# Output-projection products spread over the last steps of a first attention, gate products spread further over a second, and a weight split in two pieces

## The reference, cut to what matters

```
first block:
  xn = rms_norm(x) ; proj = xn @ w_in -> qa ka va za | qi ki wi | qb kb vb zb
  a_out = attention over the 128 keys that an indexer picks (8 heads of 64)
  b_out = dilated attention (8 heads of 64)
  mixed = concat(a_out * silu(za), b_out * silu(zb))
  x = x + mixed @ w_out
second block:
  h = rms_norm(x) ; proj = h @ w_in_2 -> q, kv, gates, pool input, g_merge
  a = nsa_attention(...) @ w_branch_attn       # compressed + selected + window
  b = pool_mixer(...) @ w_branch_pool
  ga, gb = split(sigmoid(g_merge))
  x = x + (ga * a + gb * b) @ w_out_2
  x = x + square(relu(rms_norm(x) @ w_ff1)) @ w_ff2 ; rms_norm
```

## Time and profile before

| what | before |
|---|---|
| median of 3 runs | 1055.77 us (1055.59 to 1056.2) |
| the profiled execution | 1055.27 us |
| its span, first to last instruction | 1053.5 us |
| PE busy | 1038.2 us (99% of the span) |
| DVE / ACT / POOL busy | 650.9 / 517.2 / 341.9 us (62% / 49% / 32%) |
| mean DMA rate | 139 GB/s |
| mean granted TensorE clock | 0.998 |

### The profile page before, as it was taken

The page is one execution under the profiler, slowest core; times in us unless marked ns, Lnnn a source line. Parts: engine busy times, 40 slices in busy tenths (PEclk is TensorE's granted clock), DMA queues, the critical chain, the costliest instruction groups (busy, mean ns, idle before and its releaser), DMA issues. The chain is left out here.

```text
span 1053.5 us, 14396 instructions
## 1 busy us (share of the span) xinstructions
PE 1038.2 (99%) x5362; PEld 851.5 (81%) x5362; DVE 650.9 (62%) x1149; ACT 517.2 (49%) x929; POOL 341.9 (32%) x329
## 2 busy tenths in 40 slices
PE   9999999999999999999999999999999999999997
PEld 7788887888778898988777778888888888888885
DVE  5578997676775333514567778444222325999976
ACT  8453345554562343344467874134433436554554
POOL 0022110004310003700155430008679954753542
PEclk9999999999999999999999999999999999999999
DMA  8654323223320375133200362239999942443542
GB/s 329 116 124 107 100 80 78 64 62 120 132 91 1 108 242 158 41 80 81 60 2 2 108 233 60 81 100 338 341 345 335 333 163 61 150 137 133 199 180 81
DMA packets 99639, 146.26 MB, mean 139 GB/s; under 512 B 6209, under 2 KB 60225, under 8 KB 99569
## 3 DMA queue, kind: packets, MB, share of 16 engines
q1 hardware_dynamic: 86016, 129.70, 37.9%
q10 hardware_dynamic: 12768, 12.88, 3.8%
q0 software_dynamic: 784, 2.75, 1.7%
HBM read 123.69 MB, written 21.63 MB: 138 GB/s over the span
## 5 line engine op out<-in xcount | busy, mean ns | idle before, releaser
L2319 DVE TENSOR_TENSOR w_lo<-wring,w_hi 128x1024 fp32r<-128x1024 f32 x32 | 50.6, 1582 | 110.4 <-ACT w_hi L1732 110.4
L1878 DVE TENSOR_TENSOR u_lo<-wring,u_hi 128x1024 fp32r<-128x1024 f32 (+1 forms) x64 | 78.8, 1240 | 53.0 <-ACT u_hi L1469 52.5
L842 PE MATMUL bank<-u_hi,h_hi 128*128 128x512 f32 (+1 forms) x288 | 110.9, 385 | 0.1
L842 PE MATMUL bank<-u_hi,h_lo 128*128 128x512 f32 (+1 forms) x288 | 109.2, 379 | 0.0
L842 PE MATMUL bank<-u_lo,h_hi 128*128 128x512 f32 (+1 forms) x288 | 109.0, 378 | 0.0
L1469 ACT ACTIVATE u_hi<-wring 128x1024 fp32r<-128x1024 f32 (+1 forms) x64 | 65.8, 1032 | 82.8 <-PE bank L842 70.3
L842 PE MATMUL bank<-h_hi,w_lo 128*128 128x512 f32 (+2 forms) x272 | 104.5, 384 | 0.0
L842 PE MATMUL bank<-h_hi,w_hi 128*128 128x512 f32 (+2 forms) x272 | 104.4, 384 | 0.0
L842 PE MATMUL bank<-h_lo,w_hi 128*128 128x512 f32 (+2 forms) x272 | 104.3, 384 | 0.0
L842 PE MATMUL bank<-h_hi,u_hi 128*128 128x512 f32 x224 | 95.0, 424 | 0.3 <-ACT arena L1411 0.2
L1303 PE MATMUL bank<-s_hi,f_hi 128*128 128x512 f32 x224 | 88.5, 395 | 0.1
(11 more groups left out here) (349 smaller groups left out, 2478.8 us busy)
## 6 DMA issues: line engine op xcount, KB each, us to landing
wring<-in_w_in SPq DMA_DIRECT2D x60, 512.0 KB, 3.9
wring<-in_w_ff ACTq DMA_DIRECT2D x12, 1024.0 KB, 8.5
wring<-sums_kept SPq DMA_DIRECT2D x16, 768.0 KB, 4.3
wring<-in_w_ff SPq DMA_DIRECT2D x22, 512.0 KB, 6.1
wring<-in_w_ff SPq DMA_DIRECT2D x32, 256.0 KB, 3.3
sums_kept<-wring SPq DMA_DIRECT2D x22, 256.0 KB, 5.2
arena<-in_w_out SPq DMA_DIRECT2D x4, 1024.0 KB, 5.1
wring<-in_w_out SPq DMA_DIRECT2D x2, 2048.0 KB, 13.6
```

What stands on the lines that cost most here:

```text
L842: last = mm(b, lhs, rhs, start=(start and n == 0), stop=(stop and n == 2))
L1878: v.tensor_tensor(u_lo[u % RAW_UNITS][:, 0:cols], raw_unit(u), u_hi[u % HI_UNITS][:, 0:cols].bitcast(F32), ALU.subtract).then_inc(u_lo_don ...
L2319: v.tensor_tensor(cut(w_lo[ring3(m)]), src, cut(w_hi[ring3(m)]).bitcast(F32), ALU.subtract).then_inc(w_lo_done, 1)
```

## The change

It edits five things.

1. **First attention, PE.** Sixteen products of i = 0 (eight for each half n) leave the place behind the last step. Seven of them go into the pairs t = 58 to 66 (`ROW_AT`), behind the scores and ahead of turns and values; one goes ahead of the last output's transposes, the other eight behind them, in an order that keeps those that need the last outputs late (`first_row`).
2. **First block's weight splits.** The parts 5 to 8 of `WO` get their low split on POOL, behind its last `combo`, and no longer on DVE; ACT makes their high splits earlier (59, 61, 63 and right behind the last step), and that of part 9 ahead of the last mixed high split.
3. **Gate projection of the second block.** The last products of `gb` are stretched: the last four stand in the pairs t = 52, 54, 56, 58 in place of 48, 50, 52, 54.
4. **Branch weight splits.** The high splits of e = 0 and 1 on ACT go from behind steps 59 and 62 to behind 61 and 63. The low split of e = 0 on POOL goes from u = 59 to two pieces of 512 columns, at u = 61 and at u = 63; each counts one, so a product with e now waits for e + 2.
5. **Branch products.** The last two products of `branch_product(1)` move ahead of the wait for the attention's low splits.

```diff
--- before.py
+++ after.py
@@ -190,7 +190,7 @@
     FILL2 = [("gb", e) for e in range(2, 8)]
     fill1 = [(m * 7 // 8, FILL1[m // KC], m % KC) for m in range(KC * len(FILL1))]
     GB2_FRONT = 3
-    fill2 = [(m - GB2_FRONT if m < 32 else 32 + (m - 32) * 4 // 3 if m < 44 else 2 * m - 40, FILL2[m // KC], m % KC)
+    fill2 = [(m - GB2_FRONT if m < 32 else 32 + (m - 32) * 3 // 2 if m < 44 else 2 * m - 36, FILL2[m // KC], m % KC)
              for m in range(GB2_FRONT, KC * len(FILL2))]
     filled = {tile: t for t, tile, k in fill1 if k == KC - 1}
 
@@ -199,11 +199,12 @@
 
     SILU_STEP = [filled[FILL1[2 * n + 1]] for n in range(4)]
     WO = [(0, 0, 2), (0, 2, 2), (0, 4, 1), (0, 5, 1), (0, 6, 1), (0, 7, 1)] + [(1, k, 1) for k in (4, 5, 6, 7, 0, 1, 2, 3)]
-    WO_HIGH = {46: 0, 48: 1, 50: 2, 53: 3, 55: 4, 60: 5, 62: 6}
+    WO_HIGH = {46: 0, 48: 1, 50: 2, 53: 3, 55: 4, 59: 5, 61: 6, 63: 7}
     MIXED = [4, 5, 6, 7, 0, 1, 2, 3]
+    ROW_AT = {58: ((0, 0),), 60: ((0, 1),), 62: ((0, 2),), 64: ((0, 4), (0, 5)), 66: ((0, 3), (1, 0))}
     ROUNDS = TOPK // 8 * (NT - 1)
     GB_HIGH = {9 * n + 7: unit_of[("gb", 6 + n)] for n in range(2)}
-    BRANCH_HIGH = {59: 0, 62: 1}
+    BRANCH_HIGH = {61: 0, 63: 1}
 
 
     A1 = [("qi", 0), ("qi", 1), ("ki", 0)]
@@ -1020,6 +1021,31 @@
                     last = nc.tensor.transpose(b[:, i * P:(i + 1) * P], qk1[:, o // 4, o % 4, OUTS, i * P:(i + 1) * P], ident)
                 last.then_inc(t_full, 1)
 
+            def product1(b, i, n, j):
+                k = MIXED[j]
+                at, c = mix_place(k)
+                return three(b, (wo_high_of(n, k)[:, 0, :], wo_low_of(n, k)[:, 0, :]), slice(0, 512),
+                             (qk1_half[:, at, c, MIX_HI, :], qk1_half[:, at, c, MIX_LO, :]), slice(i * P, (i + 1) * P),
+                             False, j == 0, j == KC - 1)
+
+            def row1(n, j):
+                k = MIXED[j]
+                if j == 0:
+                    pe.wait_ge(a_free, A1_END)
+                pe.wait_ge(mixed_lo_done, j + 1)
+                pe.wait_ge(wo_lo_done, [m for m, (half, c, count) in enumerate(WO) if half == n and c <= k < c + count][0] + 1)
+                return product1(bank[n][:, :], 0, n, j)
+
+            def first_row():
+                row1(1, 1)
+                mixed_transposes(NS // NH - 1)
+                row1(0, 6)
+                row1(1, 2)
+                row1(0, 7).then_inc(r_full, 1)
+                for j in range(3, KC):
+                    last = row1(1, j)
+                last.then_inc(r_full, 1)
+
             pe.wait_ge(t_free, TT[("qk", "qb", 3)] + 1)
             pe.wait_ge(rel_free, IDX_HEADS * (NT - 1))
             for t in range(0, NS + 4, 2):
@@ -1031,6 +1057,8 @@
                     pair1(t)
                     fill(fill1, t)
                     fill(fill1, t + 1)
+                for n, j in ROW_AT.get(t, ()):
+                    row1(n, j)
                 if t % NH == 2 and t >= 18:
                     mixed_transposes((t - 18) // NH)
                 for n in range(2):
@@ -1038,13 +1066,13 @@
                         turn1(t - 2 + n)
                     if 4 <= t:
                         value1(t - 4 + n)
-            mixed_transposes(NS // NH - 1)
-            pe.wait_ge(a_free, A1_END)
-            pe.wait_ge(o_free, NS // NH)
-
-            def residual(r0, ready, product, then):
+
+            def residual(r0, ready, product, then, first_row=None):
 
                 for i in range(NT):
+                    if i == 0 and first_row is not None:
+                        first_row()
+                        continue
                     for n in range(2):
                         if n == 1 and i >= 1:
                             then(i - 1)
@@ -1058,22 +1086,7 @@
 
             h2 = lambda i: h_transposes("h2", xn2, NT, [i])
 
-            def ready1(i, n):
-                if i == 0 and n == 0:
-                    pe.wait_ge(wo_lo_done, 6)
-
-            def product1(b, i, n, j):
-                k = MIXED[j]
-                at, c = mix_place(k)
-                if i == 0 and n == 0:
-                    pe.wait_ge(mixed_lo_done, j + 1)
-                if i == 0 and n == 1:
-                    pe.wait_ge(wo_lo_done, 7 + j)
-                return three(b, (wo_high_of(n, k)[:, 0, :], wo_low_of(n, k)[:, 0, :]), slice(0, 512),
-                             (qk1_half[:, at, c, MIX_HI, :], qk1_half[:, at, c, MIX_LO, :]), slice(i * P, (i + 1) * P),
-                             False, j == 0, j == KC - 1)
-
-            residual(0, ready1, product1, h2)
+            residual(0, lambda i, n: None, product1, h2, first_row)
 
 
             nat_unit("kv2", 0, tiles=[0, 1, 2])
@@ -1217,7 +1230,7 @@
 
             def branch_product(at, chunks=range(4)):
                 e, n = BRANCH[at]
-                pe.wait_ge(br_lo_done, e + 1)
+                pe.wait_ge(br_lo_done, e + 2)
                 if at >= 4:
                     pe.wait_ge(r_free, 2 * NT + at - 3)
                 act = (a_hi, a_lo) if n == 0 else (pm_hi, pm_lo)
@@ -1245,10 +1258,9 @@
                     branch_product(0)
                 if t == NS + 2:
                     branch_product(1, range(2))
+            branch_product(1, range(2, 4))
             pe.wait_ge(at_lo_done, NT - 1)
             for half in range(2):
-                if half == 1:
-                    branch_product(1, range(2, 4))
                 pe.wait_ge(last_lo_done, half + 1)
                 for at in (2, 3):
                     branch_product(at, range(2 * half, 2 * half + 2))
@@ -1592,10 +1604,11 @@
                     mixed_high((t - 19) // NH)
                 if t in WO_HIGH:
                     wo_high(WO_HIGH[t])
+            wo_high(8)
             mixed_high(6)
-            wo_high(7)
+            wo_high(9)
             mixed_high(7)
-            for m in range(8, 14):
+            for m in range(10, 14):
                 wo_high(m)
             for u in range(HI_UNITS):
                 high(U2 + u)
@@ -2071,13 +2084,14 @@
                 for u in (t, t + 1):
                     if u in LOW1:
                         low(LOW1[u])
-                    if u - 2 in WO_HIGH:
+                    if WO_HIGH.get(u - 2, 5) < 5:
                         wo_low(WO_HIGH[u - 2])
             mixed_low(6)
-            wo_low(7)
             mix(7)
+            dve.wait_ge(wo_lo_done, 9)
+            wo_low(9)
             mixed_low(7)
-            for m in range(8, 14):
+            for m in range(10, 14):
                 wo_low(m)
             for u in range(2):
                 low(U2 + u)
@@ -2290,7 +2304,7 @@
                     if u - 3 in GB_HIGH:
                         low(GB_HIGH[u - 3])
                 if t == NS:
-                    dve.wait_ge(br_lo_done, 1)
+                    dve.wait_ge(br_lo_done, 2)
                     branch_low(1)
                 if t == NS + 4:
                     gate(0)
@@ -2469,6 +2483,13 @@
                 g.tensor_tensor(combo[c % 2][:, 0:(i + 1) * P], strips[:, h, (NT - 1 - i) * P:S], mask_of[i], ALU.add)\
                     .then_inc(combo_done, 1)
 
+            for m in range(5, 9):
+                n, k, count = WO[m]
+                pool.wait_ge(wo_lo_done, m)
+                pool.wait_ge(wo_hi_done, m + 1)
+                g.tensor_tensor(wo_low_of(n, k, count), wo_raw(n, k, count), wo_high_of(n, k, count).bitcast(F32), ALU.subtract)\
+                    .then_inc(wo_lo_done, 1)
+
             pool.wait_ge(xn_done, NT)
             pool.wait_ge(r_full, R_BRANCH)
             pool.wait_ge(t_free, TT[("mx", NS // NH - 1)] + 1)
@@ -2519,10 +2540,11 @@
                         .then_inc(pm_lo_done, 1)
                 if u >= 15 and u % NH == NH - 1:
                     add_turned((u - 15) // NH)
-                if u == 59:
+                if u in (61, 63):
                     pool.wait_ge(br_hi_done, 1)
-                    g.tensor_tensor(br_lo[0][:, :], wring[:, branch_at[0]:branch_at[0] + UNIT], br_hi[0][:, :].bitcast(F32), ALU.subtract)\
-                        .then_inc(br_lo_done, 1)
+                    part = slice((u - 61) * 256, (u - 61) * 256 + 512)
+                    g.tensor_tensor(br_lo[0][:, part], wring[:, branch_at[0]:branch_at[0] + UNIT][:, part], br_hi[0][:, part].bitcast(F32),
+                                    ALU.subtract).then_inc(br_lo_done, 1)
 
             def side_totals(j):
                 pool.wait_ge(a_free, AT[("ff", 2 * j + 1)] + 1)
```

## The result

| | before | after |
|---|---|---|
| median | 1055.76 us (1055.42 to 1056.49, 6 runs) | 1060.67 us (1059.63 to 1061.46, 6 runs) |
| profiled execution, its span | 1055.27, 1053.5 | 1060.80, 1059.0 |
| mean granted clock of TensorE | 0.998 | 0.995 |

The change makes the kernel slower: the ratio is 1.0046 with an interval of 1.0034 to 1.0058, so 4.9 us (3.6 to 6.1). The prediction was 1060.0 in a range of 1056.9 to 1062.6.

The account below looks back on a forecast made before the run. PE was taken to bound the kernel, so only its idle time can be won. -1.7 (first attention) + 4.2 (second) + 1.7 (clock) = +4.2 us on 1055.27, 1059.5; median 1060.0, range 1056.9 to 1062.6.

Parts of the forecast that it names:

- first attention: End of the first attention: products fill PE's waits, 3.27 to 1.25 us; less 0.3 at the norm, 1.7 us gained.
- first branch product late: Second attention: PE waits for POOL's second piece behind output 6's addition; product starts at 617.2, not 612.46, 4.75 us late.
- wait of 0.53 filled: Second attention, at 620.12: two branch products moved ahead of the attention's low splits fill PE's wait, gain 0.53 us.
- clock: Behind the 5.9 us gap of PE: granted clock falls to half for 3.5 us, costing 1.75 us.
- those of 0.23 and twice 0.15: First attention, waits of PE left: 0.23 at t = 58, 0.15 for the transposes, 0.15 for the split of output 6.
- What the norm takes back: Norm of query block 0: block ready at 315.5, PE there at 315.2, giving back 0.3 us.
- The wait of 0.51: Second attention, at 603.66: PE's wait is filled by the stretched gate products, counted as 0.3 us.
- the 0.82: Second attention: PE's wait for POOL's scaling of steps 60 and 61 goes, as no branch split stands ahead of it.
- the rival of 0.28: Behind the same stall of PE, the clock holds or returns within a few matmuls: +2.5, 1058.3 us; chance 0.28.
- The branch weights: Rival, second attention: weights land at 609.5, ACT's chain and the second piece come 2 us later, 1062.0 us; chance 0.12.
- The short stall: Rival, second attention: ACT's chain runs on PE's lead, piece done before about 614.5, 1055.0 or 1053.5 us; chance 0.08.
- That the first attention gives nothing: Rival: DVE's chain sets the first attention's end, gain 0 and not 1.7, so 1061.7 us; chance 0.07.

Follow-up runs that it names:

- the first part alone: Points 1 and 2 of the change only, second attention, its fill work and branch splits as before: 1054.03 us, 0.9984 to the kernel before.
- the two kernels with one of the two undone: Points 1 and 2 only, against 1054.03 us: low splits 5 to 8 back on DVE, 1054.26 us; or no first-row products among the attention's steps, 1055.61 us.
- the second part alone: Points 3, 4 and 5 of the change only, first attention as before: 1061.99 us, 1.0060 to the kernel before.
- the unused matmuls: Changed kernel with 24 matmuls of 128 by 512, results never used, ahead of the first branch product: 1059.58 us, 1.0038 to the kernel before.
- the kernel with the short gap: Changed kernel with POOL's second piece of the branch split ahead of the addition of output 6: 1056.17 us, 1.0002 to the kernel before.

## Why the prediction was right

The mechanism was the one forecast: the stall, what it waits for, the clock behind it and the smaller gain ahead. The sizes of its terms compare so:

| term | predicted | measured |
|---|---|---|
| first attention | -1.7 | -1.64 by medians, -2.14 between the profiled executions |
| first branch product late | +4.75 | +5.23 |
| wait of 0.53 filled | -0.53 | gone from the trace |
| clock | +1.75 | +2.04 in the trace, 1.1 by medians |

By the traces this sums to +4.6, against the +4.2 forecast and +4.9 by medians. The late product and the clock cost 0.48 and 0.29 us more than forecast, and the first attention gave 0.44 more, so the errors cancel in part: that the total came within 0.7 us is in part luck.

- *First attention.* The waits went from 3.27 to 0.57, further than the 1.25 predicted: those of 0.23 and twice 0.15 that I left standing are not there, and the last one is 0.57 for 0.72. Of these 2.70 us, 2.22 reach the second row of products (1.38 earlier, 0.84 late at the start); no wait in the profile names the rest. What the norm takes back is not fixed by this code: of the seven traces with this first row, four have no wait at the norm, as the changed kernel's, and three one of 0.25 to 0.42. That is why the first part alone gives 1.64 in its trace (0.86 early at the norm, 0.78 late at the start) and the same code 2.14 in the other. That the products and not the splits do it is shown by the two kernels with one of the two undone.
- *The late branch product.* The order on POOL was read rightly: the sum on DVE, the addition, 0.72 us and not the 1.72 of the earlier trace rows, then 1.26 for the piece. Put on the frame of before (1.30 added), the addition began at 615.6 and not at 615.1, and that is the half microsecond by which the term was too small. Of it 0.29 stands already at DVE's sum (614.31 for 614.02), since ACT's chain did not hold its place as forecast but came that much later; 0.30 lies between that sum and the addition (1.29 from start to start for 0.99), and is 0.99 again in the second part alone, without a cause that the traces show. PE arrived at 612.0 and not at 611.3. The wait of 0.51 was filled whole, but 0.58 of the 0.82 stayed. The forecast took all of it to come from the split ahead of POOL's scaling; with no split ahead, that scaling (606.92) stands 1.33 us for DVE's reciprocals. Both together are 0.4 of the 0.7 us, and no wait names the rest. The idle time was therefore 5.66 and not 5.9. When PE arrives does not change when the product starts: POOL sets that alone. The exchange of the two pieces shows it, worth 7.4 us with the clock.
- *The clock.* It fell, as against the rival of 0.28. I had taken 3.5 us at half clock, as long as the fall took, which no row showed; PE worked 4.3 us at half clock here, and less in the traces of two other kernels (twelve matmuls in 4.28 and 4.21 us for 4.84). By the medians the term is smaller, 1.1 us, so the nearness of 1.75 is partly luck. With the clock held by the unused matmuls the kernel took 1059.6, where the rival had 1058.3.
- *Rivals.* The branch weights were not late: ACT has no wait for them. The short stall needed the piece by 614.5; it came at 616.24, or 617.5 on the frame of before. That the first attention gives nothing is refuted by the first part alone, 1.64 us faster.

## What to carry to other kernels

When a split or copy is cut into pieces, each piece takes its place in an in-order queue. Here the first reader read only half of the columns, and it was the half that was made last: give the first reader the first piece, and look at what stands ahead of each. A gap of the bounding engine can cost more than its length, by the matmuls behind it that run at half clock: one of 2.06 us did so here, in the profiled execution and, by the mean clock, in six of the ten others. And before filling a wait, follow the engine that ended it to its next deadline: there it may come back in full.

## What the runs showed of the hardware

The granted clock fell from 2.4 to 1.2 GHz 3.1 us after PE's last matmul in the changed kernel (at 613.9), and 5.0 us after it in the second part alone (at 617.9, the gap beginning at 612.9). It fell after a gap of only 2.06 us too, 3.3 us after that gap began, with PE at work for 1.3 us already; I had expected a gap shorter than the time to the fall to be safe. The low stretch was 6.8 us long behind the gap of 5.66 and 3.4 us behind those of 5.37 and 2.06, so the loss differs between kernels that are nearly alike, and between executions of one: the kernel with the short gap ran from 1054.51 (mean clock 0.998) to 1057.28 (0.996). The Trainium skill (TensorE: Matmul & The Clock Gate, What's actually happening) says of the release at a kernel's start that its moment varies between runs, with a phase that the kernel does not set. That the moment varies agrees with the falls here, 3.1, 5.0 and 3.3 us after the gap began; no run here shows a phase.

POOL's addition of 128x256 took 0.72 to 0.74 us in the three traces where DVE was idle beside it, and 1.42 to 1.73 in the nine where DVE's branch split of 128x1024 ran beside it (1.43 with the pieces exchanged, 1.72 in the earlier trace rows). Where it is 1.7 the row begins 0.3 earlier: from the start of DVE's sum to the end of the addition it is 2.71 us in both cases, and 2.01 in the changed kernel. The Trainium skill (GPSIMD Engine Reference, Specifications) has POOL share its SBUF interfaces with VectorE instructions of two SBUF inputs, and the split is one. The numbers agree. In the changed kernel DVE's split waits for POOL's second piece, so the two do not meet there.
